# One-column modulation products placed singly between chunks of split products, and the rope key of mixer 1 worked as split products

## What is computed

```
mod  = jnp.split(jax.nn.silu(c)     @ w_mod[l] + b_mod[l], N_MOD, axis=-1)   # 6 x 1024
modc = jnp.split(jax.nn.silu(c_ctx) @ w_mod[l] + b_mod[l], N_MOD, axis=-1)
h    = modulate(rmsnorm(x, norm1_g[l]), mod[0][:, None], mod[1][:, None])
...
proj = u @ w_in
cq, ckv, kr, dq, dk, dv, g = jnp.split(proj, ...)        # kr: 32 columns, the rope key
k_rope = rope(kr[:, :, None, :], positions, MLA_THETA, MLA_ROPE)
```

## Time and profile before

| | us |
|---|---|
| median of 3 runs | 1275.31 (1274.98 to 1278.06) |
| span of the profiled execution | 1275.3 |
| TensorE busy | 1215.8 |
| VectorE busy | 837.7 |
| ScalarE busy | 632.1 |
| GpSimd busy | 534.4 |

### The profile page before, as it was taken

The page is one execution under the profiler, slowest core; times in us unless marked ns, Lnnn a source line. Parts: engine busy times, 40 slices in busy tenths (PEclk is TensorE's granted clock), DMA queues, the critical chain, the costliest instruction groups (busy, mean ns, idle before and its releaser), DMA issues.

```text
span 1275.3 us, 24245 instructions
## 1 busy us (share of the span) xinstructions
PE 1215.8 (95%) x9052; PEld 1137.3 (89%) x9052; DVE 837.7 (66%) x1146; ACT 632.1 (50%) x1008; POOL 534.4 (42%) x283
## 2 busy tenths in 40 slices
PE   6999998998999999999999999998899898999998
PEld 6999998976888999999999888977677798999998
DVE  6888875865964577776555843688737685655555
ACT  5444445616651554444435545566417535555553
POOL 0354336632451534334535644478430473232331
PEclk9999998999999999999989999999999998999999
DMA  8677863433333457777504323233212254555553
GB/s 318 234 262 283 281 216 104 149 116 117 116 100 118 163 199 248 279 278 266 181 32 149 125 90 133 84 100 99 83 67 100 83 165 133 185 181 183 186 182 105
DMA packets 58095, 207.03 MB, mean 162 GB/s; under 512 B 6576, under 2 KB 8240, under 8 KB 57776
## 3 DMA queue, kind: packets, MB, share of 16 engines
q1 hardware_dynamic: 49824, 177.23, 40.6%
q0 software_dynamic: 6912, 25.17, 5.4%
q10 hardware_dynamic: 1296, 3.74, 0.8%
HBM read 205.07 MB, written 1.05 MB: 162 GB/s over the span
## 4 chain that ended last, share of the span: by engine, by line
PE 79%; DVE 8%; ACT 4%; issue 4%; POOL 3%; DMA 1%; DVEq 0%; SPq 0%; POOLq 0%; ACTq 0%
PE psum L609 22%; PE psum L610 21%; PE psum L611 21%; PE psum L949 2%; POOL own_parts L2786 2%; PE psum L620 1%; POOL high L2869 1%; PE psum L622 1%; PE psum L621 1%; DMA low<-stream 1%; PE psum L743 1%; DVE parts L2074 1%; PE psum L897 1%; PE psum L663 1%; PE psum L634 1%
## 5 line engine op out<-in xcount | busy, mean ns | idle before, releaser
L609 PE MATMUL psum<-parts 128*128 128x256 f32 x1584 | 452.1, 285 | 17.3 <-DVE parts L2074 9.9
L610 PE MATMUL psum<-parts 128*128 128x256 f32 x1584 | 450.7, 285 | 0.0
L611 PE MATMUL psum<-parts 128*128 128x256 f32 x1584 | 450.6, 284 | 0.0
L609 PEld LDWEIGHTS psum<-parts 128*128 128x128 f32 x1584 | 306.8, 194 | 18.5 <-issue 15.7
L2794 POOL TENSOR_TENSOR parts<-low,parts 128x1024 fp32r<-128x1024 f32 x60 | 158.4, 2640 | 362.4 <-ACT parts L1429 362.4
L610 PEld LDWEIGHTS psum<-parts 128*128 128x128 f32 x1584 | 306.9, 194 | 0.0
L611 PEld LDWEIGHTS psum<-parts 128*128 128x128 f32 x1584 | 306.6, 194 | 0.0
L1429 ACT ACTIVATE parts<-low 128x1024 fp32r<-128x1024 f32 x198 | 207.9, 1056 | 177.8 <-DMA low<-stream 177.0
L2786 POOL TENSOR_TENSOR own_parts<-low,parts 128x1024 fp32r<-128x1024 f32 x76 | 188.0, 2487 | 197.3 <-ACT parts L1498 197.1
L2074 DVE TENSOR_TENSOR parts<-low,parts 128x1024 fp32r<-128x1024 f32 x138 | 164.8, 1218 | 23.3 <-ACT parts L1429 22.0
L611 PE MATMUL psum<-scratch_parts,own_parts 128*128 128x256 f32 (+1 forms) x496 | 150.2, 303 | 0.0
(11 more groups left out here) (355 smaller groups left out, 2198.2 us busy)
## 6 DMA issues: line engine op xcount, KB each, us to landing
low<-stream SPq DMA_DIRECT2D x334, 512.0 KB, 3.5
high<-conditioning POOLq DMA_DIRECT2D x48, 512.0 KB, 5.1
high<-wuq ACTq DMA_DIRECT2D x1, 1152.0 KB, 11.0
low<-x SPq DMA_DIRECT2D x4, 256.0 KB, 5.8
high<-ctx ACTq DMA_DIRECT2D x1, 1024.0 KB, 5.7
out<-low SPq DMA_DIRECT2D x8, 128.0 KB, 1.8
low<-cst ACTq DMA_DIRECT2D x1, 850.5 KB, 5.4
low<-vec ACTq DMA_DIRECT2D x1, 157.5 KB, 5.8
```

The source lines that it names most:

```text
L609: pe.matmul(out, w_hi[:, cols_], x_hi, start=start, stop=False, **kw)
L610: pe.matmul(out, w_hi[:, cols_], x_lo, start=False, stop=False, **kw)
L611: return pe.matmul(out, w_lo[:, cols_], x_hi, start=False, stop=stop, **kw)
```

## The change

Three things, all in the order or the form of work; the amount of modulation work stays the same.

1. Where the one-column products stand. `split_cols` and `context_side` take a function `beside` that is called behind each chunk. The 24 products of mixer 1 go singly behind the 24 chunks of dq1, dq2 and dq3; the 16 of mixer 2 behind the 16 chunks of the context sides of rows and mk0; the last 8 behind the chunks of mq0. The wait for the context's modulation (`mod_ready`, 2) moves ahead of rows.
2. The rope key. ScalarE writes the upper part of `wkr` near the end of FFN 1, VectorE the lower part, and the key is 24 split products with 32 weight columns from the mixer's split input. Its result lies in rows 0 to 31 of the bank, and VectorE reads it there.
3. The whole copy of the input (`input_whole`, eight activations) falls away, and with it the wait for it.

```diff
-            def split_cols(t, out, hi, lo, chunk_ready=lambda k: None):
+            def split_cols(t, out, hi, lo, chunk_ready=lambda k: None, beside=lambda k: None):
                 w = split_weights(t)
                 for k in range(DC):
                     chunk_ready(k)
                     mm = split_product(out, w, slice(k * P, (k + 1) * P), (hi(k), lo(k)), k == 0, k == DC - 1)
+                    if k < DC - 1:
+                        beside(k)
                 mm.then_inc(S("tiles_used"), 1)
+                beside(DC - 1)
...
-            split_project("dq1")
+            def modulation_beside(k, who, first):
+
+                return lambda c_: modulation(k, who, first + c_, first + c_ + 1)
+
+            split_project("dq1", beside=modulation_beside(0, 0, 0))
             spread("q_norm")
-            split_project("dq2")
+            split_project("dq2", beside=modulation_beside(0, 0, DC))
...
-            split_project("dq3")
-            modulation(0, 0, 0, 24)
+            split_project("dq3", beside=modulation_beside(0, 0, 2 * DC))
             spread("kv_norm")
             bank_free(pe, "kr")
-            pe.wait_ge(S("small_weights"), 32)
+            pe.wait_ge(S("rope_weights_split"), 1)
             for k in range(DC):
-                pe.wait_ge(S("input_whole_1"), k + 1)
-                mm = pe.matmul(bank("kr")[64:96, 0:T], wkr[:, k, :], u1[:, k, :], start=k == 0, stop=k == DC - 1)
+                mm = split_product(bank("kr")[0:ROPE_D, 0:T], (wkr_hi, wkr_lo), slice(k * ROPE_D, (k + 1) * ROPE_D),
+                                   (p1_hi[:, k, :], p1_lo[:, k, :]), k == 0, k == DC - 1)
...
+            pe.wait_ge(S("mod_ready"), 2)
             bank_free(pe, "rows")
-            context_side("rows")
+            context_side("rows", beside=modulation_beside(1, 0, 0))
             bank_free(pe, "mk0")
-            context_side("mk0")
-            pe.wait_ge(S("mod_ready"), 2)
-            modulation(1, 0, 0, 16)
+            context_side("mk0", beside=modulation_beside(1, 0, DC))
...
-            modulation(1, 0, 16, 24)
...
-            for n in range(4):
+            split_project("mq0", None, *lat_parts, beside=modulation_beside(1, 0, 2 * DC))
+            for n in range(1, 4):
                 split_project(f"mq{n}", None, *lat_parts)
...
+                    act.wait_ge(S("small_weights"), 32)
+                    act.activation(wkr_hi, wkr, ACT.Copy).then_inc(S("rope_weights_upper"), 1)
...
-            for n in range(4):
-                input_whole(n)
...
-            for n in range(4, DC):
-                input_whole(n)
...
+            dve.wait_ge(S("rope_weights_upper"), 1)
+            dve.tensor_tensor(wkr_lo, wkr, wkr_hi, ALU.subtract).then_inc(S("rope_weights_split"), 1)
```

More of the change, by code:

```diff
@@ L443, in two_blocks @@
         cq, ckv, kr = A1("cq", 3), A1("ckv", 2), A1("kr")
-        wuq, wkr = A1("wuq", 3), A1("wkr", 8)
+        wuq, wkr = A1("wuq", 3), A1("wkr")
+        wkr_hi, wkr_lo = u_parts[:, 0:DC * ROPE_D], u_parts[:, DC * ROPE_D:2 * DC * ROPE_D]
         w_nope = place(ARENA_1["p"][0], 3 * HEADS * NOPE).rearrange("p (k b) -> p k b", k=3)
@@ L767, in _ @@
             spread("ffn1_post")
-            u1k = lambda k: u1[:, k, :]
-            def project(name, out=None, rhs=u1k, **kw):
-                bank_free(pe, name)
-                cols(tile_of(name), bank(name)[:, 0:T] if out is None else out, rhs, **kw)
             def split_project(name, out=None, hi=lambda k: p1_hi[:, k, :], lo=lambda k: p1_lo[:, k, :], **kw):
@@ L987, in side_chunk, with context_side @@
                                      k == 0, k == DC - 1)
-            def context_side(name, first=0, last=DC):
+            def context_side(name, first=0, last=DC, beside=lambda k: None):
                 for k in range(first, last):
@@ L1533, in _ @@
             act.dma_start(wuq, dram["wuq"]).then_inc(S("small_weights"), 16)
-            act.dma_start(wkr, dram["wkr"]).then_inc(S("small_weights"), 16)
+            act.dma_start(A1("wkr", 8), dram["wkr"]).then_inc(S("small_weights"), 16)
             take_root("ffn1_pre", D)
@@ L1580, in keep_latent @@
                     copy_bank(name, to[:, n, :])
-            def input_whole(n):
-                act.activation(u1[:, n, :], h[:, n, :], ACT.Identity, scale=v("mix_pre", n)).then_inc(S("input_whole_1"), 1)
             keep_latent("cq0", 0, cq, 2)
@@ L2280, in _ @@
             product_ready(dve, "kr")
-            dve.tensor_tensor(kr[64:96, :], bank("kr")[64:96, 0:T], inv_mix[64:96, :], ALU.mult).then_inc(read_done("kr"), 1)
+            dve.tensor_tensor(kr[64:96, :], bank("kr")[0:ROPE_D, 0:T], inv_mix[0:ROPE_D, :], ALU.mult).then_inc(read_done("kr"), 1)
             all_rows, mla_rows = slice(0, P), slice(64, 96)
```

## The result

The changed kernel takes 1290.85 us (median of 6 runs, 1280.72 to 1291.92) where the kernel before takes 1276.79 (6 runs, 1274.98 to 1280.64). The ratio is 1.0087, 95% interval 1.0064 to 1.0111: 11 us. The two medians lie 14.1 us apart and the spans of the two profiled executions 13.3 (1288.6 us against 1275.3).

A forecast was written before the change was run, and what follows sets the result against it. TensorE, busy 95% of the span, was taken to bound the kernel, with its clock deciding. Terms 0 + 5.6 + 3.7 + 1.6 - 0.4 = +10.5 us on 1275.3 gave 1285.8 us, range 1273 to 1288.

The forecast's parts named there:

- The price of a single: Anywhere on TensorE: a one-column product costs 0.22 to 0.23 us at full clock, 0.42 at the low one.
- rows and mk0, +5.6: Mixer 2's context sides: chunks with one-column products at low clock take 16.9 us together against 11.3, +5.6 us.
- low from end to end: Mixer 2, rows and mk0: the clock is low at the start and the mix never wins it back, 16.9 us together.
- mq0, +3.7: Mixer 2, mq0: clock falls about 0.5 us in and stays low, so +3.7 us against 4.47 now.
- mq1 +1.6: Mixer 2, mq1: begins at low clock and needs a closed run to win it back, +1.6 us.
- the wait ahead of mq2 -0.4: Mixer 2, between mq1 and mq2: the present wait of TensorE goes, -0.4 us.
- Mixer 1, 0 us (-0.9 to +0.8): Mixer 1: an 0.85 us gain, limited by VectorE's key read, set against a possible clock fall; 0 us net.
- half of 1.6: Mixer 1, wait ahead of rdq0: the clock may fall once, at worst 1.6 us; half of it was counted.
- Holding the clock in dq1 to dq3: Mixer 1, dq1 to dq3: the mix of chunks and one-column products should hold a clock that is already high.
- The third rival: Mixer 1, dq1 to dq3: high clock not held, +0.8 us added to other cases; no chance of its own.
- The first, that the mix wins the clock back: Mix wins the clock back as closed chunks do, then nothing falls: -2.4 us, 1272.9 us; chance 0.22.
- the second as well: Mixer 2: clock comes back in rows or mk0 but not in mq0, +1.9 us, 1277.2 us; chance 0.16.

## Why the prediction was right, step by step

Forecast +10.5 us, measured +11 by the ratio (8 to 14); the direction held, and so did the mechanism of mixer 2, on which all of the 10.5 rested. That the sum came so close is in part luck: between the two traces mixer 2 gave +9.1 where 10.5 was forecast, mixer 1 +3.2 where 0 was, and 1.1 us came from a stretch that was in no term. In plain numbers the median of the changed kernel's runs, 1290.85, lies 2.9 us above the top of the range. The range counted from 1275.3, the kernel before stood at 1276.8 in the second set of runs, and its upper end gave mixer 1 no more than +0.8. Nor is mixer 2 as before equally long in every trace: the one of the kernel before shows 54.0 us from the first spread to the turn product, five traces of kernels with the same mixer 2 show 52.2 to 52.6, and the changed kernel 63.1. Against those five mixer 2 costs 10.5 to 10.9 us, and with mixer 1's 3.2 that is about the 14 between the medians.

- **The price of a single** (0.22 to 0.23 at full clock, 0.42 at the low one): right. 0.58 per chunk and single is 0.353 + 0.225; 1.07 is 0.64 + 0.42.
- **rows and mk0, +5.6:** right in kind, a little too large. From norm1's first spread to its second it was +4.4 in the trace after and +4.6 with this part alone. The step that was off is "low from end to end": the clock was still 1.00 as rows began and fell at about 647.5, a microsecond in. The prediction had taken over the state of the profiled execution before, where it fell ahead of rows.
- **mq0, +3.7, mq1 +1.6, the wait ahead of mq2 -0.4:** together +4.9, measured +4.6 from the second spread to the turn product. mq0 took 8.6 us (691.04 to 699.68) where 8.2 were expected; mq1 with the wait behind it took 3.9 where it had taken 3.3, so 0.7 more and not 1.2. mq0 began behind a wait of 2.29 us, as expected from the 1.84 + 0.60 of before.
- **Mixer 1, 0 us (-0.9 to +0.8):** wrong, +3.2. dk0 ended where it was expected (255.8, forecast 256.5), and the key took 2.9 us (of its gain only 0.7 was the form's, the rest the full clock's). The failed step is that the read of the key was taken as fixed at 259.2 to 259.6, because "VectorE has nothing in its queue that the change takes away there". That is true of the queue and says nothing of how long its operations take. The read depends on GpSimd, whose work depends on when ScalarE makes an upper, and that on the end of dk0. It came 1.95 us later in relation to the spread. The second mis-sized term is the clock, of which I took half of 1.6: it fell for certain in a wait of 5.2 us, and rdq0 with dk1 took 5.7 us where they had taken 3.7. 1.1 us later and 2.1 slower make the 3.2.
- **Holding the clock in dq1 to dq3:** right, 1.00 from 226 to 249. The third rival did not occur. The first, that the mix wins the clock back, is refuted by 14.9 us of mix at 0.50 in rows and mk0 (647.6 to 662.5); the second as well, since it did not come back there either. That the prediction gave the first a chance of 0.22 was fair on the rows of before, none of which showed a mix at low clock.
- **What was not in the sum:** +1.1 us at FFN 2's start, of which the change touches nothing; all ten other kernels have it too.

The Trainium skill's rule (TensorE: Matmul & The Clock Gate, Why this matters for your kernels) was to keep the engine continuously busy. The traces here disagree with it as far as singles go: from 647.6 to 668 there is no gap, and the clock stays at half, 14.9 us of it in the mix.

## What to carry to other kernels

Put thin products (one column) only where the clock is already full and wide work surrounds them, and put closed wide work first wherever the clock may have fallen; the same mix costs 0.58 or 1.07 us per step by that alone. Here this was seen stage by stage; no change of mixer 2 alone shortened the whole kernel clear of its scatter. Before an engine is made to arrive earlier, follow what its end releases on the others: here an earlier dk0 gave GpSimd work that blocked the very VectorE chain TensorE then waited for, and moving five small operations behind the awaited read was worth 6.5 us at the place. And ask of a row of thin work what wait it hides before it is taken out.

## What was not expected of the hardware

- A VectorE operation of 128x4 took 0.17 or 2.26 us, and where it took long it ended within 0.04 us of the end of a GpSimd operation on SBUF. The one of 128x16 ahead of it took 2.0 to 2.1 us in six traces, while those of 128x1 took 0.15 to 0.21, beside GpSimd's work or not. So a small operation on a chain that others wait for can cost the rest of a GpSimd operation.
- One and the same mix ran at 1.00 in one execution of a kernel and at 0.50 in other kernels and, by their time, in its other executions: 1275.6 against 1284.9 to 1287.7 us. A work list that can only hold the clock makes the time depend on what stood before it.
- Low stretches far from any edit differ between traces: the one near 1004 us is 3.4 us long in some and 10.2 in others. With the mix one tile later, most of a lead of 2.1 us that stood behind mixer 2 was lost there. What decides it was not settled; single stretches are therefore compared here before totals.
